# Three unsplit weight pieces of layer 0 become split ones, with their low parts made by ScalarE and an adding DMA

## The chip, the cores and the metric

The kernel runs on one core of a Trainium2 chip. The metric is the device time of one execution in microseconds; less is better. TensorE (PE in the profile) multiplies, VectorE (DVE) and ScalarE (ACT) do the elementwise work, GpSimd (POOL) and SyncE (SP) issue DMAs, and POOL adds up a few bias maps.

## The reference

Two layers of a decoder trunk on x of 256 tokens by 1024 features, in float32. Each layer:

```
mod = silu(c) @ w_mod[layer] + b_mod[layer];  shift, scale, gate = split(mod, 3)
hdn = rms_norm(x, norm_w[layer]) * (1 + scale) + shift
q1, k1, v1, g1, q2, k2, v2, g2 = split(hdn @ w_in[layer], 8)
y1, y2 = two attention branches (layer 0: differential and dilated; layer 1: block-sparse and stick-breaking)
y = concat([y1 * silu(g1), y2 * silu(g2)]) @ w_out[layer]
x = x + gate * y
```

The projections (ten column groups of 512 in each layer, K1, Q1, V1, K2, Q2, V2, G1, G2 and the two halves O0, O1 of the output) are most of TensorE's work.

## The kernel before

**Pieces and steps.** The weights are cut into 80 pieces, each 128 partitions by 1024 float32 (two blocks of 128 rows by 512 columns, 512 KB). A layer is 80 steps of TensorE. A step multiplies one piece with one half (side 0 or 1) of the activations, and most pieces are used in two steps. In layer 0, steps 24 to 31 are K2, 32 to 39 Q2, 40 to 47 V2, 48 to 55 G1, 56 to 63 G2 and 64 to 79 the output. Piece 12 + i belongs to steps 24 + 2i and 25 + 2i as far as piece 27; so piece 23 is used in steps 46 and 47 (V2, its last part), piece 25 in 50 and 51, piece 26 in 52 and 53 (both G1). Between the steps TensorE does the attention: scores of a pair of maps, transposes into the PSUM bank `turned`, products into the bank `mixed`.

**Split and plain pieces.** A split piece exists twice, as `w_hi` (rounded to fp32r) and `w_lo` (the rest); `mm3` (called in `project`) multiplies hi with hi, hi with lo and lo with hi, three fp32r matmuls. A piece in `PLAIN` is multiplied as it was loaded (`raw`) by one float32 matmul, which the profile shows as two. `split_hi(n)` (L478) lets ScalarE copy `raw` to `w_hi`, `split_lo(n)` (L751) lets VectorE subtract `w_hi` from `raw`. `w_hi` and `w_lo` have 8 slots each, which the pieces of `SPLIT` take in turn; `split_before(n)` is the one that held the slot. The copy is placed at the end of ScalarE's work for step `hi_at(n)`: 8 steps ahead of the first use, or as many as `EARLY` says, or in a step of `CHANGE_HI`. The subtraction stands in VectorE's work one step later (`lo_at`).

**What sets the order.** Every engine's program is unrolled step by step, each engine runs its own list in order, and semaphores connect them. ScalarE's list for step g begins with the copies out of `turned` (`take_turned`, L537 to L548) and `mixed` that TensorE filled in step g - 1, then come the exponentials of the attention maps (`exp_map`, L581), the squares of a finished group, and at its end the copies to `w_hi`. TensorE may not write `turned` again before ScalarE has emptied it (`turned_left`, L1090). The two transposes of K2 come after steps 36 and 37 (`TURN_QK`, L165), those of the normed heads (`turn_subln`) after steps 52 and 53 (`SUBLN_AT`).

**Loads.** SP issues one queue of loads into a ring of `RAW` = 7 buffers: pieces and 48 tiles of `w_mod`, which VectorE multiplies and sums in `take_mod` (L771), in the steps of `MOD_AT` (L180). The list is sorted (L404 and L405): a split piece by `hi_at`, a plain one by its first step, a `w_mod` tile by its step less one. Load i waits until the content of load i - 7 has been used: a `w_mod` tile by `take_mod`, a plain piece by the last of its steps, a split piece by `split_lo`. SP takes them strictly in this order. Four plain pieces (`HELD`) are instead loaded by POOL into `qT` and `kT` after step 59.

## Time and profile before

| | us |
|---|---|
| three runs, median | 324.62 |
| lowest and highest | 324.25, 324.77 |
| the profiled execution, its own time | 324.23 |
| its span, first to last instruction | 322.4 |

The profiled execution has 1.8 us outside its span and lies 0.4 us under the median. Busy are PE 299.4 us, DVE 235.2, ACT 196.9, POOL 16.2; TensorE's granted clock was 0.997 of full over the span. In a row of a timeline the first number is the start, the second the length from the first start to the last end of the merged instructions, and what stands in brackets is the idle time of the engine ahead of it and what ended that. A row of the chain of work gives start and length of a stretch on the path that ended last.

### The profile page before, as it was taken

How to read it: one execution, taken by the hardware profiler on the slowest of the kernel's cores; microseconds unless marked ns; L12 is line 12 of the kernel's file. 1: busy time of each engine (PE TensorE's matmuls, PEld its weight loads, DVE VectorE, ACT ScalarE, POOL GpSimd, SP SyncE). 2: the span in 40 equal slices, each digit the busy share in tenths (PEclk: the TensorE clock that was granted, in tenths of full speed). 3: DMA queues.
4: the chain of work that ended last, by engine and by line, in shares of the span. 5: the costliest groups of instructions: out<-in, count | busy, mean ns of one | idle time of the engine just before them, and what ended most of it. 6: DMA issues, size and time to landing. Idle time of an engine off the chain costs nothing.

```text
span 322.4 us, 4790 instructions
## 1 busy us (share of the span) xinstructions
PE 299.4 (93%) x1709; PEld 237.6 (74%) x1709; DVE 235.2 (73%) x480; ACT 196.9 (61%) x401; POOL 16.2 (5%) x24
## 2 busy tenths in 40 slices
PE   3498998999998999989999999999999999899995
PEld 2476876777555688886576888888987799798783
DVE  3898999998886697698957457989773547638633
ACT  3625568736745687998256446556664798959400
POOL 0000000000000942020000000000000000000000
PEclk9999999999999999999999999999999999999998
DMA  7999999495678958688752315679547148000011
GB/s 253 363 401 411 405 406 399 147 328 180 248 265 255 332 203 317 216 329 320 260 196 65 133 65 195 209 256 305 209 155 277 48 143 273 23 0 2 0 67 65
DMA packets 19879, 70.31 MB, mean 218 GB/s; under 512 B 2192, under 2 KB 2576, under 8 KB 19856
## 3 DMA queue, kind: packets, MB, share of 16 engines
q1 hardware_dynamic: 19280, 67.91, 58.4%
q0 software_dynamic: 576, 2.10, 1.7%
q8 instruction: 14, 0.23, 0.3%
q14 instruction: 9, 0.07, 0.1%
HBM read 68.95 MB, written 1.05 MB: 217 GB/s over the span
## 4 chain that ended last, share of the span: by engine, by line
PE 68%; DVE 12%; ACT 9%; DMA 5%; issue 3%; SPq 1%; ACTq 0%; DVEq 0%
PE proj L1082 46%; PE score L1082 13%; DMA raw<-in_w 5%; PE mixed L1082 5%; DVE raw L771 4%; DVE w_lo L751 3%; PE turned L1127 2%; ACT w_hi L478 2%; PE turned L1109 2%; DVE y L946 1%; DVE gt L938 1%; DVE probs L1021 1%; ACT y L502 1%; ACT gt L627 1%; SPq L449 1%
## 5 line engine op out<-in xcount | busy, mean ns | idle before, releaser
L751 DVE TENSOR_TENSOR w_lo<-raw,w_hi 128x1024 fp32r<-128x1024 f32 x68 | 82.3, 1222 | 14.1 <-ACT w_hi L478 13.6
L478 ACT ACTIVATE w_hi<-raw 128x1024 fp32r<-128x1024 f32 x68 | 70.6, 1050 | 17.8 <-DMA raw<-in_w 16.7
L1082 PE MATMUL proj<-w_hi,hy_hi 128*128 128x512 f32 x144 | 60.0, 417 | 4.8 <-DVE hy_lo L805 4.4
L771 DVE CUSTOM_DVE_ANT_0 raw<-raw,c_rows 128x1024 f32<-128x1024 f32 x48 | 59.0, 1251 | 0.0
L1082 PE MATMUL proj<-w_lo,hy_hi 128*128 128x512 f32 x144 | 56.9, 395 | 0.0
L1082 PE MATMUL proj<-w_hi,hy_lo 128*128 128x512 f32 x144 | 56.8, 394 | 0.0
L1082 PE MATMUL proj<-hy_hi,w_hi 128*128 128x256 f32 x176 | 52.5, 298 | 0.0
L1082 PE MATMUL proj<-hy_lo,w_hi 128*128 128x256 f32 x176 | 49.7, 283 | 0.0
L1082 PE MATMUL proj<-hy_hi,w_lo 128*128 128x256 f32 x176 | 49.7, 283 | 0.0
L1082 PEld LDWEIGHTS proj<-w_hi,hy_hi 128*128 128x128 f32 x144 | 27.5, 191 | 13.0 <-issue 3.9
L1082 PEld LDWEIGHTS proj<-hy_hi,w_hi 128*128 128x128 f32 x176 | 33.6, 191 | 2.1 <-issue 2.1
L1082 PEld LDWEIGHTS proj<-hy_lo,w_hi 128*128 128x128 f32 x176 | 33.6, 191 | 0.2 <-issue 0.2
L1082 PEld LDWEIGHTS proj<-hy_hi,w_lo 128*128 128x128 f32 x176 | 33.6, 191 | 0.0
L1082 PEld LDWEIGHTS proj<-w_hi,hy_lo 128*128 128x128 f32 x144 | 27.5, 191 | 6.1
L1082 PEld LDWEIGHTS proj<-w_lo,hy_hi 128*128 128x128 f32 x144 | 27.6, 191 | 5.4 <-issue 0.5
L581 ACT ACTIVATE probs<-logits,stat 128x128 f32<-128x128 f32 (+1 forms) x48 | 21.3, 446 | 6.7 <-DVE stat L853 6.7
L1082 PE MATMUL proj<-raw,y 128*128 128x512 f32 x48 | 22.4, 595 | 0.0
L548 ACT ACTIVATE probsT<-turned 128x384 f32<-128x384 f32 x20 | 9.7, 483 | 17.9 <-PE turned L1127 17.9
L890 DVE TENSOR_REDUCE n_ms<-sq 128x8 f32<-128x512 f32 (+1 forms) x13 | 9.4, 726 | 11.3 <-ACT sq L615 9.8
L1021 DVE SCALAR_TENSOR_TENSOR probs<-score,logits 128x384 f32<-128x384 f32 x8 | 4.1, 552 | 17.0 <-ACT logits L692 17.0
L1082 PE MATMUL score<-w_hi,hy_hi 128*128 128x512 f32 x40 | 16.1, 402 | 0.0
L1082 PE MATMUL score<-w_lo,hy_hi 128*128 128x512 f32 x40 | 15.6, 390 | 0.0
(147 smaller groups left out, 439.8 us busy)
## 6 DMA issues: line engine op xcount, KB each, us to landing
raw<-in_w SPq DMA_DIRECT2D x76, 512.0 KB, 4.7
raw<-in_w_mod SPq DMA_DIRECT2D x48, 512.0 KB, 5.7
xs<-in_x SPq DMA_DIRECT2D x1, 1024.0 KB, 5.2
qT<-in_w POOLq DMA_DIRECT2D x2, 512.0 KB, 6.5
kT<-in_w POOLq DMA_DIRECT2D x2, 512.0 KB, 8.4
out_x<-xs SPq DMA_DIRECT2D x4, 256.0 KB, 2.0
cst<-in_constants SPq DMA_DIRECT2D x1, 520.0 KB, 6.3
logits<-in_a_lambda SPq DMA_DIRECT2D x1, 128.0 KB, 12.1
```

The costliest lines, as they stand in the source:

```text
L449: sp.dma_start(raw_tile(key), whence.rearrange("p (k n) -> p k n", k=2)).then_inc(raw_full[i % RAW], 16)
L478: nc.scalar.activation(w_hi[:, slot(n), :, :], raw_tile(("w", n)), ACT.Copy).then_inc(hi_done, 1)
L502: j = nc.scalar.activation(y[:, k, :], b[:, i * S:(i + 1) * S], ACT.Identity, scale=v[:, V_A + k:V_A + k + 1], bias=v[:, V_B + k:V_B + k + 1])
L548: nc.scalar.activation(probsT[:, (2 * j + o) % 4, :], turned[:, 0:MAPW], ACT.Copy).then_inc(turn_act, 1)
L581: i = nc.scalar.activation(probs[:, M % 4, cs], logits[:, M % 2, cs], ACT.Exp, scale=-1.0, bias=st[:, tile:tile + 1], accum_out=st[:, 2 + ...
L751: nc.vector.tensor_tensor(w_lo[:, slot(n), :, :], raw_tile(("w", n)), w_hi[:, slot(n), :, :], ALU.subtract).then_inc(lo_done, 1)
L771: nc.vector.tensor_tensor_reduce(out=tile, in0=tile, in1=c_rows[:, :], scale=1.0, scalar=0.0, op0=ALU.mult, op1=ALU.add, accum_out=col(V_M ...
L890: nc.vector.reduce_sum(n_ms[:, n % 2, heads * s:heads * s + heads], src.rearrange("p (h d) -> p h d", h=heads), axis=AX.X).then_inc(ms_ok, 1)
L1021: nc.vector.scalar_tensor_tensor(out=probs[:, (2 * i + o) % 4, :], in0=score[o][:, 0:MAPW], scalar=0.0, in1=logits[:, o, :], op0=ALU.max, ...
L1082: return nc.tensor.matmul(o, a, b, start=start, stop=stop, skip_group_check=True)
L1109: i = nc.tensor.transpose(turned[:, b * P:(b + 1) * P], qn[:, s, b * P:(b + 1) * P], ident)
L1127: i = nc.tensor.transpose(turned[:, b * P:(b + 1) * P], probs[:, (2 * j + o) % 4, b * P:(b + 1) * P], ident)
```

## The change

- Pieces 23, 25 and 26 leave `PLAIN` and become split pieces; a new list `SUMMED` names them. Their copies to `w_hi` are placed by `SUMMED_HI` in the steps 33, 36 and 37.
- Their low part is not made by VectorE. Right behind the copy, ScalarE waits for it and writes `w_lo` = -`w_hi` (a second copy with scale -1). POOL waits for that (`neg_ok`) and issues a DMA that reads the piece once more from HBM and adds it into `w_lo` (`accum_op` add). Three such DMAs stand at the start of POOL's list. TensorE waits for the landing (`summed_in`) instead of for VectorE.
- SP may refill the ring buffer of such a piece once its `w_hi` copy is done.
- In `EARLY`, three entries change: the high part of piece 27 moves from step 38 to 41, that of 28 from 43 to 45, that of 29 from 45 to 47 (with three more split pieces each slot comes free later). Their subtractions on VectorE move along, from 39, 44 and 46 to 42, 46 and 48.
- The keys by which loads are sorted change with it: 23, 25 and 26 are loaded at places 40, 45 and 47 of the queue (before 57, 61 and 64), and the entries between move back. The plain piece 19, used from step 38 on, goes from place 45 to 48, so from behind the release of load 38 (the `w_mod` tile of step 30) to behind that of load 41, which now is the `w_mod` tile of step 35. Piece 20 goes from 48 to 50, 21 from 51 to 54, 22 from 54 to 56.

```diff
--- before.py
+++ after.py
@@ -68,7 +68,10 @@
 
 HELD = (34, 37, 38, 39)
 HELD_FROM = 59
-PLAIN = (18, 19, 20, 21, 22, 23, 25, 26, 34, 37, 38, 39)
+PLAIN = (18, 19, 20, 21, 22, 34, 37, 38, 39)
+
+SUMMED = (23, 25, 26)
+SUMMED_HI = (33, 36, 37)
 SPLIT = [n for n in range(len(FIRST)) if n not in PLAIN]
 
 
@@ -86,6 +89,11 @@
     return SPLIT.index(n) + 1
 
 
+def lo_count(n):
+
+    return sum(m not in SUMMED for m in SPLIT[:SPLIT.index(n) + 1])
+
+
 def done_at(layer, c, side):
 
     return STEPS * layer + max(g for g, (cc, p, s) in enumerate(STEP[layer]) if (cc, s) == (c, side))
@@ -109,7 +117,7 @@
 
 
 
-EARLY = {24: 14, 27: 16, 28: 13, 29: 12, 30: 10, 31: 9, 32: 12, 33: 11, 35: 12, 36: 10,
+EARLY = {24: 14, 27: 13, 28: 11, 29: 10, 30: 10, 31: 9, 32: 12, 33: 11, 35: 12, 36: 10,
          72: 12, 73: 12, 74: 12, 75: 11, 78: 4, 79: 4}
 
 CHANGE_HI = {40: 67, 41: 68, 42: 69, 43: 70, 44: 74, 45: 76, 46: 79, 47: 80}
@@ -119,6 +127,8 @@
 def hi_at(n):
     if n < 12:
         return FIRST[n] - 6
+    if n in SUMMED:
+        return SUMMED_HI[SUMMED.index(n)]
     return CHANGE_HI.get(n, max(FIRST[n] - EARLY.get(n, 8), LAST[split_before(n)] + 1))
 
 
@@ -132,7 +142,7 @@
 
 
 def pieces_lo(layer, g):
-    return [n for n in SPLIT if lo_at(n) == STEPS * layer + g]
+    return [n for n in SPLIT if n not in SUMMED and lo_at(n) == STEPS * layer + g]
 
 
 
@@ -394,6 +404,8 @@
         y_ok, y_hi_ok, y_lo_ok = sem("y_ok"), sem("y_hi_ok"), sem("y_lo_ok")
         upd, out_ok, stored = sem("upd"), sem("out_ok"), sem("stored")
         dve_step = sem("dve_step")
+        neg_ok = sem("neg_ok")
+        summed_in = [sem(f"summed_in{i}") for i in range(len(SUMMED))]
         held_in = [sem(f"held_in{i}") for i in range(len(HELD))]
 
 
@@ -443,8 +455,10 @@
                         n = was[1]
                         if n in PLAIN:
                             wait_step(sp, LAST[n])
+                        elif n in SUMMED:
+                            sp.wait_ge(hi_done, split_count(n))
                         else:
-                            sp.wait_ge(lo_done, split_count(n))
+                            sp.wait_ge(lo_done, lo_count(n))
                 whence = w_mod[mods.index(key[1])] if key[0] == "mod" else w[key[1]]
                 sp.dma_start(raw_tile(key), whence.rearrange("p (k n) -> p k n", k=2)).then_inc(raw_full[i % RAW], 16)
                 if key == ("w", 2):
@@ -476,6 +490,10 @@
                 if split_before(n) is not None:
                     wait_step(act, LAST[split_before(n)])
                 nc.scalar.activation(w_hi[:, slot(n), :, :], raw_tile(("w", n)), ACT.Copy).then_inc(hi_done, 1)
+                if n in SUMMED:
+                    act.wait_ge(hi_done, split_count(n))
+                    nc.scalar.activation(w_lo[:, slot(n), :, :], w_hi[:, slot(n), :, :], ACT.Copy,
+                                         scale=-1.0).then_inc(neg_ok, 1)
 
             def h_hi(n, blocks, ts):
 
@@ -1061,6 +1079,10 @@
 
         @block.gpsimd
         def _(pool):
+            for i, n in enumerate(SUMMED):
+                pool.wait_ge(neg_ok, i + 1)
+                nc.gpsimd.dma_start(w_lo[:, slot(n), :, :], w[n].rearrange("p (k n) -> p k n", k=2),
+                                    accum_op=ALU.add).then_inc(summed_in[i], 16)
             pool.wait_ge(cst_in, 16)
             wait_turned(pool, ("qk", 0, Q2, 1))
             for M in range(8, 16):
@@ -1269,8 +1291,10 @@
                 if at == FIRST[n]:
                     if plain:
                         wait_raw(pe, ("w", n))
+                    elif n in SUMMED:
+                        pe.wait_ge(summed_in[SUMMED.index(n)], 16)
                     else:
-                        pe.wait_ge(lo_done, split_count(n))
+                        pe.wait_ge(lo_done, lo_count(n))
                 if p == 0:
                     was = before_in_bank(layer, c, s)
                     if was:
```

ScalarE from behind the seed of K2's norm (end of step 33) to the end of step 38, before. `L537 kT<-turned` are the two copies that empty `turned` after K2's two transposes:

```order
L561 ACTIVATE gt<-mixed,stat 128x128 x2
L478 ACTIVATE w_hi<-raw 128x1024
L548 ACTIVATE probsT<-turned 128x384
L581 ACTIVATE probs,stat<-logits,stat 128x128
L581 ACTIVATE probs,stat<-logits,stat 128x256
L537 ACTIVATE kT<-turned,v 128x4x128
L581 ACTIVATE probs,stat<-logits,stat 128x128
L581 ACTIVATE probs,stat<-logits,stat 128x256
L537 ACTIVATE kT<-turned,v 128x4x128
L561 ACTIVATE gt<-mixed,stat 128x128 x2
L478 ACTIVATE w_hi<-raw 128x1024
```

The same stretch now, where L492 is `w_hi`, L495 the new `w_lo<-w_hi`, L555 the copy to `kT`:

```order
L492 ACTIVATE w_hi<-raw 128x1024
L495 ACTIVATE w_lo<-w_hi 128x1024
L579 ACTIVATE gt<-mixed,stat 128x128 x2
L492 ACTIVATE w_hi<-raw 128x1024
L566 ACTIVATE probsT<-turned 128x384
L599 ACTIVATE probs,stat<-logits,stat 128x128
L599 ACTIVATE probs,stat<-logits,stat 128x256
L492 ACTIVATE w_hi<-raw 128x1024
L495 ACTIVATE w_lo<-w_hi 128x1024
L555 ACTIVATE kT<-turned,v 128x4x128
L599 ACTIVATE probs,stat<-logits,stat 128x128
L599 ACTIVATE probs,stat<-logits,stat 128x256
```

and on, without a gap:

```order
L492 ACTIVATE w_hi<-raw 128x1024
L495 ACTIVATE w_lo<-w_hi 128x1024
L555 ACTIVATE kT<-turned,v 128x4x128
L579 ACTIVATE gt<-mixed,stat 128x128 x2
L633 ACTIVATE sq<-proj2 128x512
```

Six instructions have come in: a pair ahead of `gt<-mixed`, a pair ahead of the first `kT<-turned`, a pair ahead of the second. The `w_hi` copy of piece 27, which stood behind the second `gt<-mixed`, has gone.

ScalarE in steps 47 to 50, before. `L607 val<-proj1` ends the V2 group, `L471` ends the seed for the normed heads:

```order
L607 ACTIVATE val<-proj1 128x512
L581 ACTIVATE probs,stat<-logits,stat 128x128
L581 ACTIVATE probs,stat<-logits,stat 128x256
L467 ACTIVATE n_y<-n_ms,v 128x8
L469 ACTIVATE n_y<-n_y 128x8
L471 ACTIVATE n_t<-n_y 128x8
L478 ACTIVATE w_hi<-raw 128x1024
L590 ACTIVATE probs<-probs,stat 128x128
L590 ACTIVATE probs<-probs,stat 128x256
L590 ACTIVATE probs<-probs,stat 128x128
```

and now:

```order
L492 ACTIVATE w_hi<-raw 128x1024
L625 ACTIVATE val<-proj1 128x512
L599 ACTIVATE probs,stat<-logits,stat 128x128
L599 ACTIVATE probs,stat<-logits,stat 128x256
L481 ACTIVATE n_y<-n_ms,v 128x8
L483 ACTIVATE n_y<-n_y 128x8
L485 ACTIVATE n_t<-n_y 128x8
L492 ACTIVATE w_hi<-raw 128x1024
L608 ACTIVATE probs<-probs,stat 128x128
L608 ACTIVATE probs<-probs,stat 128x256
L608 ACTIVATE probs<-probs,stat 128x128
```

The `w_hi` copy of piece 29 has come in between the square of `gt` and `val<-proj1`.

## Rows read from the trace of the kernel before

**Rows 1.** The page's first section: busy us, share, instructions of each engine.
```profile
PE 299.4 (93%) x1709; PEld 237.6 (74%) x1709; DVE 235.2 (73%) x480; ACT 196.9 (61%) x401; POOL 16.2 (5%) x24
```
**Rows 2.** Chain that ended last, steps 37 to 39: start us, us, what.
```profile
82.88 1.72 PE proj L1082 x4
84.60 0.44 PE turned L1109 x4
85.03 0.67 PE mixed L1082 x6
85.70 3.44 PE proj L1082 x8
```
**Rows 3.** Timeline of ACT, 76 to 86 us: start us, us, engine, line, what, [idle before].
```profile
76.65 0.62 ACT L561 ACTIVATE gt<-mixed,stat 128x128 f32<-128x128 f32 x2
77.17 1.06 ACT L478 ACTIVATE w_hi<-raw 128x1024 fp32r<-128x1024 f32 x1
80.76 0.49 ACT L548 ACTIVATE probsT<-turned 128x384 f32<-128x384 f32 x1 [2.53 <-PE turned L1127]
82.58 0.40 ACT L581 ACTIVATE probs<-logits,stat 128x128 f32<-128x128 f32 x1 [1.33 <-DVE stat L853]
...
83.48 0.67 ACT L537 ACTIVATE kT<-turned,v 128x512 f32<-128x512 f32 x1
...
85.07 0.69 ACT L537 ACTIVATE kT<-turned,v 128x512 f32<-128x512 f32 x1
```
**Rows 4.** Timeline of DVE, 79 to 82 us.
```profile
79.63 1.22 DVE L751 TENSOR_TENSOR w_lo<-raw,w_hi 128x1024 fp32r<-128x1024 f32 x1
80.77 1.22 DVE L771 CUSTOM_DVE_ANT_0 raw<-raw,c_rows 128x1024 f32<-128x1024 f32 x1
```
**Rows 5.** Timeline of all engines, 99.3 to 100.4 us.
```profile
99.38 0.69 ACT L537 ACTIVATE qT<-turned,v 128x512 f32<-128x512 f32 x1 [0.61 <-PE turned L1109]
...
100.21 0.41 PE L1127 MATMUL turned<-cst,probs 128*128 128x128 f32 x2 [0.87 <-ACT qT L537]
```
**Rows 6.** Timeline of SP's issues, and, for `raw` at 60 to 100 us, issue to landing.
```profile
72.04 5.29 SPq L449 DMA_DIRECT2D raw<-in_w  x2
82.02 0.33 SPq L449 DMA_DIRECT2D raw<-in_w_mod  x1
```
```profile
DMA to landing us min/median/max: 3.3/4.5/6.7
```
**Rows 7.** Chain that ended last: a split step by tokens, a plain and a split by columns.
```profile
60.73 1.39 PE proj L1082 x6
...
120.81 1.73 PE proj L1082 x8
...
218.53 1.44 PE proj L1082 x12
```
**Rows 8.** Timeline of ACT, 110 to 122 us (steps 47 to 53).
```profile
111.29 0.58 ACT L607 ACTIVATE val<-proj 128x512 f32<-128x512 f32 x1
...
113.36 1.04 ACT L478 ACTIVATE w_hi<-raw 128x1024 fp32r<-128x1024 f32 x1
114.30 1.48 ACT L590 ACTIVATE probs<-probs,stat 128x128 f32<-128x128 f32 x4
...
117.98 0.40 ACT L581 ACTIVATE probs<-logits,stat 128x128 f32<-128x128 f32 x1 [0.87 <-DVE stat L853]
...
121.07 0.67 ACT L542 ACTIVATE y<-turned,v 128x512 f32<-128x512 f32 x1
```
**Rows 9.** Timeline of DVE, 113 us.
```profile
113.48 0.17 DVE L756 SCALAR_TENSOR_TENSOR n_t<-n_ms,n_t 128x8 f32<-128x8 f32 x1 [0.54 <-ACT n_t L471]
```
**Rows 10.** Chain that ended last: the two transposes of the normed heads.
```profile
120.37 0.44 PE turned L1119 x4
...
122.54 0.44 PE turned L1119 x4
```
**Rows 11.** DMA issues by line: engine op xcount, KB each, median us to landing.
```profile
qT<-in_w POOLq DMA_DIRECT2D x2, 512.0 KB, 6.5
kT<-in_w POOLq DMA_DIRECT2D x2, 512.0 KB, 8.4
```

## The prediction

> **What bounds the kernel now.** I read the page's shares first: TensorE is busy 93% of the span, the next engine 73% [rows 1], and the clock was 0.997. A change pays if it shortens TensorE's work where TensorE is the last to be ready, and it costs wherever it lets TensorE wait. So next I read the chain of work around the places that the change touches. From step 37 on it is one unbroken TensorE stretch: projection, transpose of K2, product, projection, each starting where the one before ends [rows 2]. Every microsecond that TensorE waits there is a microsecond of the kernel, since ScalarE and VectorE take their later work from TensorE. Then I read what ScalarE does in the same time, to see how much room it has [rows 3]: it is idle for 2.53 us before 80.76 and for 1.33 us before 82.58, in the second case because VectorE's logits are not there. Then comes the row that matters most: `kT<-turned` starts at 83.48, and TensorE's next transpose, which needs that bank empty, at 84.60. The room is below one microsecond.
>
> **The gain: shorter steps.** The pieces 23, 25 and 26 feed steps 46, 47 and 50 to 53. A plain step takes 1.72 us by tokens [rows 2] and 1.73 by columns, a split one 1.39 and 1.44 [rows 7]. That is 2 x 0.33 + 4 x 0.29 = 1.82 us less TensorE work. VectorE gets none of it, since the low parts are made elsewhere.
>
> **The cost in steps 33 to 38: two copies per piece on ScalarE.** A copy to `w_hi` takes 1.06 us [rows 3]. The negation has the same shape and I give it the same time: the first of the pair must end before it starts (1.06, and 0.03 for the wait), the second lets its successor start 0.1 before its end, so a pair costs 1.06 + 0.03 + 0.95 = 2.04 us. The replay, in times of the trace:
> - Pair 23 (step 33) goes ahead of `gt<-mixed`, which started at 76.65, and the copy of piece 24, which started at 77.17 [rows 3]. That copy now runs 79.19 to 80.25. The idle 2.53 us behind it take this in for ScalarE and for `probsT` at 80.76, but VectorE subtracts piece 24 from 79.63 on [rows 4] and now must wait to 80.27: 0.64 us late. VectorE has no gap ahead of the next logits, so ScalarE's exponentials start at 83.2 instead of 82.58.
> - Pair 25 (step 36) stands behind these exponentials and ahead of the first `kT<-turned`. 82.58 + 0.64 + 0.90 (the exponentials: 83.48 - 82.58) = 84.12; pair to 86.16; so the copy starts at 86.16 instead of 83.48.
> - TensorE starts 0.83 us after the start of such a copy (99.38 to 100.21, where it did wait for one) [rows 5]. So the second K2 transpose starts at 86.99; in the chain TensorE was ready at 84.60, and its first row in the timeline is some 0.15 before that. Against 84.43 the loss is 2.56 us. Without VectorE's delay (if it caught up) it would be 1.92: that is the lower end.
> - Pair 26 (step 37) delays the second `kT<-turned` to about 89.7, but TensorE needs `turned` again only after steps 38 and 39, at 89.14 + 2.56 = 91.7. This one is hidden, by the 3.44 us of projections [rows 2]. With the cover gone it would cost up to its 2.04.
>
> Nothing absorbs the 2.56 later: ScalarE and VectorE wait for TensorE's transposes and scores after 90 us, and none of them gets them earlier. The moved copy of 27 (38 to 41) lies in ScalarE's idle time and costs nothing; 28 takes the place of 29 in step 45.
>
> **The cost in steps 47 to 53: piece 29 moved.** Its `w_hi` copy now stands in step 47, in front of `val<-proj1`, which started at 111.29 [rows 8]. Back to back it costs 0.95. ScalarE had no gap from there to 116.6: `val`, exponentials, the seed, the copy of 30, `probs`, the copy of 31. Its one gap, 0.87 us before 117.98, is a wait for VectorE's logits, and VectorE in turn had waited for ScalarE's seed at 113.48 [rows 9] and then worked without a gap. So the gap moves along and hides nothing. ScalarE starts this run 0.33 us earlier, since step 46 is 0.33 shorter; the net is 0.62 late. Its copy of the normed heads out of `turned` starts at 121.07 + 0.62 = 121.69 [rows 8], TensorE's second transpose of them at 121.69 + 0.83 = 122.52. Before, it started at 122.54 [rows 10]. TensorE would by then have been 0.66 + 4 x 0.29 = 1.82 us ahead, and stands where it stood: the whole gain of the short steps is spent waiting for ScalarE. What is late next is ScalarE, no longer TensorE's arithmetic. I take 0.0 for this stretch. Bounds: if ScalarE were not in the way, -1.82; if the second gap were lost too, +0.3.
>
> **The adding DMAs.** The trace has no such DMA. The nearest rows are POOL's plain loads of the same 512 KB, 6.5 and 8.4 us to landing [rows 11]. The negations end near 78.8, 86.2 and 89.7, the users start at 106, 113 and 118 plus the shift: over 25 us of room each, three times those rows. I take 0. The other end: each us beyond the room costs one.
>
> **The queue of loads.** Piece 19 was issued at 72.04; now it goes behind the release of the `w_mod` tile that VectorE takes at 80.77 [rows 4, 6], which frees the buffer at 82.02 (the issue that waited for it before), 82.66 with VectorE's 0.64. With 3.3 to 6.7 us to landing [rows 6] it is there at 86.0 to 89.4. Step 38 began at 85.70 and begins, after the loss at K2, at 88.26. So at the median, 4.5 (87.2), it is just hidden by the wait for ScalarE; at the upper end it adds 1.1 us. The two do not add up, the larger counts. Without ScalarE's delay it would cost 0.3 to 3.7 us alone, so taking that wait away would not give it all back. Pieces 20 to 22 have a few us more.
> In the Trainium skill, DMA: Bandwidth & Descriptors, under Issuing engines are not separate DMA queues, DMAs of all issuing engines run on the same 16 DMA engines and interleave. By that the first adding DMA, in flight from about 79 on, would lengthen this very load, and the sum would go to its upper end, +1.1; no row here shows the two side by side.
>
> **Sum.** 324.23 (profiled execution: span 322.4 and 1.8 around it) + 2.56 + 0.0 = 326.8. The median of the runs lies 0.4 above the profiled one, so I forecast 327.1 us, slower by 0.8%.
>
> **Rivals.**
> 1. Piece 19 is the last to be ready, not ScalarE: 327.1 + 1.1 = 328.2, up to 329.5 if the adding DMA holds it up longer than any load in [rows 6]. For it: a load moved from 12 us ahead to a few. Against: the median just fits.
> 2. Part of the gain survives: if VectorE gives back its 0.64 and half of the 1.82 is kept in steps 46 to 53, 327.1 - 0.64 - 0.9 = 325.6. For it: the stretch of [rows 8] is tied together by gaps of tenths of a us.
> 3. Faster: the gain comes through and ScalarE is not late at K2. That is the case if the first `kT<-turned` starts before 84.60 - 0.83 = 83.8. It needs pair 25 to run inside the 1.33 us gap before 82.58, but the list has the pair behind the exponentials, and piece 19 would still cost its 0.3 us. Price: 324.6 - 1.82 + 0.3 = 323.1. The mechanism decides at one point and the order speaks against it.
> 4. The adding DMAs land later than 25 us: TensorE waits at step 46, 330 or more.
>
> **How the numbers follow.** Forecast 0.58 (326.2 to 327.8), rival 1 0.16, rival 2 0.12, rival 3 0.10, rival 4 0.04. The likeliest gives 327.1. The range takes in the forecast, rival 1 and most of rival 2: 325.3 to 329.0. A measurement of this kernel tells about 0.2% (0.65 us) from no change: rival 2 gives 0.07 of its 0.12 to no change and 0.05 to slower; the faster side is rival 3. So faster 0.11, same 0.08, slower 0.81.
>
> **What would show it.** In the changed kernel's profile TensorE should be idle for some 2.5 us ahead of the second transpose of K2 (near 87 us), released by ScalarE's `kT` copy, and ScalarE's rows ahead of it should be exponentials, `w_hi`, `w_lo`, `kT`. If the release is a DMA ahead of a float32 projection instead, rival 1 holds. Steps 46, 47 and 50 to 53 should be 0.3 us shorter, with TensorE's new waits at `turned` between steps 50 and 53 adding up to about as much. The forecast is wrong if the negation takes much less than 1.06 us, if `kT` starts near 84, or if no new wait appears between 115 and 125 us.

## The result, and the profile after

| | before | changed |
|---|---|---|
| runs | 4 | 4 |
| median, us | 324.67 | 333.80 |
| lowest and highest, us | 324.25, 324.77 | 331.56, 335.56 |
| the profiled execution, its own time, us | 324.23 | 335.56 |
| its span, us | 322.4 | 333.8 |

The changed kernel is slower by 2.8%: the ratio of the times is 1.0282, with a 95% interval of 1.0251 to 1.0313. The direction was forecast; the size was not. 333.8 us lies well above the range of 325.3 to 329.0. A second set of runs of the same kernel (`r_after`, below) gave 333.59 against 324.52 us.

The profiled execution is the longest of its four. The spans of the two profiles differ by 11.4 us, the medians by 9.1. I come back to that difference below.

The page's first section of the changed kernel, which answers to [rows 1]; TensorE is busy 2.7 us longer, although its arithmetic got less, because part of it ran at the lower clock, as shown below:

```profile
PE 302.1 (91%) x1729; PEld 239.4 (72%) x1729; DVE 235.5 (71%) x480; ACT 202.5 (61%) x407; POOL 19.7 (6%) x27
```

The granted clock of that span is 0.983, where it was 0.997. Line numbers have moved: L1104 is the projection that was L1082, L1131 the transposes of K2 and Q2, L1149 those of the probabilities, L1141 those of the normed heads, L555 the copy out of `turned`. Here is TensorE's timeline of the stretch from step 36 to step 42 (start us, us, engine, line, what, and in brackets the idle time ahead of it and what ended that). It answers to [rows 2], where no row waits:

```profile
84.64 0.60 PE L1131 MATMUL turned<-cst,qn 128*128 128x128 f32 x4
85.08 1.88 PE L1104 MATMUL proj<-raw,y 128*128 128x512 f32 x4
89.22 0.63 PE L1131 MATMUL turned<-cst,qn 128*128 128x128 f32 x4 [2.26 <-ACT kT L555]
89.69 0.83 PE L1104 MATMUL mixed<-val,probsT 128*128 128x128 f32 x6
90.36 5.29 PE L1104 MATMUL proj<-raw,y 128*128 128x512 f32 x8
...
96.82 3.60 PE L1104 MATMUL proj<-raw,y 128*128 128x512 f32 x8
100.26 0.83 PE L1104 MATMUL mixed<-val,probsT 128*128 128x128 f32 x6
103.85 3.53 PE L1104 MATMUL proj<-raw,y 128*128 128x512 f32 x4 [2.76 <-DMA raw<-in_w]
107.17 1.24 PE L1104 MATMUL mixed<-cst,v 128*128 128x128 f32 x8
108.25 1.88 PE L1104 MATMUL proj<-raw,y 128*128 128x512 f32 x4
```

Four things are in these rows. The wait for ScalarE's `kT` is the forecast one. Behind it eight projections take 5.29 us, where the same eight take 3.60 a few us later. Then TensorE waits 2.76 us for a load, that of piece 21 (step 42). Behind that wait four projections take 3.53 us, where four take 1.88. The two long rows are the engine's lower clock. These are windows of 4 us (window; busy us of PE, PEld, DVE, ACT, POOL; granted clock; DMA share; GB/s):

```profile
88.00:92.00 4.00, 2.78 (x13) 1.78 (x14) 1.95 (x5) 3.97 (x9) 0.88 (x1) 0.81 0.94 345
92.00:96.00 4.00, 4.00 (x13) 1.73 (x13) 1.02 (x3) 1.68 (x4) 0.86 (x1) 0.76 0.97 234
96.00:100.00 4.00, 4.00 (x17) 1.99 (x14) 2.30 (x11) 2.95 (x12) 0.00 (x0) 1.00 1.07 275
...
104.00:108.00 4.00, 4.00 (x10) 1.98 (x11) 4.00 (x8) 0.00 (x0) 0.00 (x0) 0.57 0.74 262
```

A mean of 0.5 would be the lower level, 1.2 GHz, throughout; 0.57 is nearly that.

The chain of work that ended last says the same with its own words (start us, us, what):

```profile
86.47 0.96 ACT w_hi L492
...
87.45 0.05 ACT w_lo L495
...
88.41 0.67 ACT kT L555
...
92.73 11.07 DMA raw<-in_w
103.80 0.04 issue
103.85 3.53 PE proj L1104 x4
```

The load of piece 21 took 11.1 us from issue to landing; no `raw` load issued between 60 and 100 us took more than 6.7 before [rows 6]. What the DMA engines did meanwhile is in the DMA view of 80 to 107 us (queue: packets, MB, share of 16 engines). Before, and then changed:

```profile
DMA packets 1935, 7.10 MB, mean 263 GB/s; under 512 B 206, under 2 KB 206, under 8 KB 1933
q1 hardware_dynamic: 1933, 7.07, 75.2%
```
```profile
DMA packets 2173, 7.94 MB, mean 294 GB/s; under 512 B 239, under 2 KB 239, under 8 KB 2171
q1 hardware_dynamic: 1739, 6.34, 63.6%
q0 software_dynamic: 432, 1.57, 31.5%
```

Queue q0 is POOL's: the three adding DMAs, 1.57 MB in 432 packets. The time of their packets is 31.5% of what the 16 engines have in 27 us, or 8.5 us of all 16. SP's 6.34 MB take 63.6%, 17.2 us. So a MB costs 5.4 us by adding and 2.7 us by plain loads, and the engines are now 95% busy where they were 75%. By line, the adding DMAs land after this many us at the median, against 6.5 and 8.4 of the plain ones [rows 11]:

```profile
w_lo<-in_w POOLq DMA_DIRECT2D x3, 512.0 KB, 9.3
```

**Where the 11.4 us of the two profiles lie.** For each step I took the time at which TensorE's last matmul of the step signals, subtracted that of the profile of before, and noted by how much this delay grows between two marks (positive is slower). The waits for `kT` at the second K2 transpose fall into column 38, those for piece 21 into 42–45:

| kernel | to 37 | 38 | 39–41 | 42–45 | 46–47 | 48–50 | 51–54 | rest | sum |
|---|---|---|---|---|---|---|---|---|---|
| changed | 2.37 | 4.06 | 0.09 | 4.72 | -0.65 | -0.29 | 1.11 | 0.01 | 11.4 |
| `r_after` | 1.13 | 2.45 | 0.00 | 7.34 | -0.65 | -0.28 | 1.11 | -0.01 | 11.1 |
| `e_plain_dma` | 0.86 | 4.11 | 0.00 | 0.27 | -0.65 | -0.28 | 1.12 | -0.02 | 5.4 |
| `e_no_neg` | 0.03 | 1.62 | 1.78 | 6.45 | -0.65 | -0.29 | 1.11 | -0.01 | 10.0 |
| `e_dve_low` | 1.06 | 1.96 | 0.00 | 1.71 | -0.65 | -0.28 | 1.11 | 0.01 | 4.9 |
| `e_29_back` | 0.10 | 2.47 | 0.00 | 6.17 | -0.65 | -0.29 | 0.28 | 0.01 | 8.1 |
| `e_late_add` | 1.05 | 2.46 | 0.00 | 0.97 | -0.65 | -0.28 | 3.61 | -0.03 | 7.1 |
| `v_add` | 0.81 | 0.00 | 4.10 | 0.00 | -0.64 | -0.28 | 0.28 | 0.03 | 4.3 |
| `v_plain_placed` | 0.54 | 0.00 | 1.91 | 0.00 | -0.66 | -0.28 | 1.63 | 0.08 | 3.2 |
| `v_add_late` | 0.13 | 0.00 | 0.00 | 1.60 | -0.66 | -0.28 | 3.48 | 0.01 | 4.3 |
| `v_dve_placed` | 0.28 | 0.00 | 0.00 | 0.25 | -0.65 | -0.28 | 4.74 | 0.07 | 4.4 |
| `v_g1_add` | -0.02 | 0.00 | 0.00 | 0.00 | 4.67 | -0.29 | -0.53 | 0.00 | 3.8 |
| `v_g1_dve` | 0.70 | 0.00 | 0.00 | 0.00 | 1.43 | -0.30 | -0.16 | 0.01 | 1.7 |
| `v_two` | 0.46 | 0.00 | 0.00 | -0.65 | -0.66 | 0.01 | 1.34 | 0.00 | 0.5 |
| `e_early_only` | 0.89 | 0.00 | 0.00 | 0.00 | 0.00 | 0.00 | 0.45 | 0.03 | 1.4 |

The first column is not the change. It arises before step 24, while the first loads arrive, and scatters from -0.02 to 2.37 us over kernels that are alike there; the two profiles of the same changed kernel differ by 1.24 in it. The other columns of the changed kernel sum to 9.04 us, close to the 9.1 of the medians; those of `r_after` sum to 9.97, where its medians differ by 9.07. Both profiles are of the longest of their four executions, so a single profile fixes these sums to about 1 us only. Behind step 54 nothing happens: the delay is only carried along.

### The profile page after: what moved, and what is told of

Same layout as the page of the kernel before. It is cut to its first block, busy times and chain, and to the rows that moved or that the text cites. A ratio compares the mean times of both kernels' runs of the same rounds, so it can differ in the third digit from the quotient of the medians.

```text
span 333.8 us, 4842 instructions
## 1 busy us (share of the span) xinstructions
PE 302.1 (91%) x1729; PEld 239.4 (72%) x1729; DVE 235.5 (71%) x480; ACT 202.5 (61%) x407; POOL 19.7 (6%) x27
## 3 DMA queue, kind: packets, MB, share of 16 engines
HBM read 70.52 MB, written 1.05 MB: 214 GB/s over the span
## 4 chain that ended last, share of the span: by engine, by line
PE 55%; ACT 14%; DMA 13%; DVE 11%; issue 4%; SPq 1%; ACTq 0%; DVEq 0%
PE proj L1104 36%; DMA raw<-in_w 13%; PE score L1104 12%; PE mixed L1104 4%; ACT w_hi L492 3%; DVE w_lo L769 3%; DVE raw L789 2%; ACT probs L599 2%; PE turned L1149 2%; PE turned L1131 1%; DVE y L964 1%; DVE gt L956 1%; DVE logits L871 1%; SPq L463 1%; DVE probs L1039 1%
## 5 line engine op out<-in xcount | busy, mean ns | idle before, releaser
L492 ACT ACTIVATE w_hi<-raw 128x1024 fp32r<-128x1024 f32 x71 | 73.7, 1049 | 19.2 <-DMA raw<-in_w 18.0
L1104 PE MATMUL proj<-w_hi,hy_hi 128*128 128x512 f32 x148 | 61.6, 416 | 5.6 <-DVE hy_lo L823 5.2
L1104 PE MATMUL proj<-w_lo,hy_hi 128*128 128x512 f32 x148 | 58.5, 395 | 0.0
L1104 PE MATMUL proj<-w_hi,hy_lo 128*128 128x512 f32 x148 | 58.5, 395 | 0.0
L1104 PE MATMUL proj<-hy_hi,w_hi 128*128 128x256 f32 x192 | 56.8, 296 | 0.0
L1104 PE MATMUL proj<-hy_lo,w_hi 128*128 128x256 f32 x192 | 54.2, 282 | 0.0
L1104 PE MATMUL proj<-hy_hi,w_lo 128*128 128x256 f32 x192 | 54.2, 282 | 0.0
L1104 PEld LDWEIGHTS proj<-w_hi,hy_hi 128*128 128x128 f32 x148 | 28.2, 190 | 14.3 <-issue 4.5
L1104 PEld LDWEIGHTS proj<-hy_hi,w_hi 128*128 128x128 f32 x192 | 36.6, 191 | 1.9 <-issue 1.9
L1104 PEld LDWEIGHTS proj<-hy_lo,w_hi 128*128 128x128 f32 x192 | 36.7, 191 | 0.0
L1104 PEld LDWEIGHTS proj<-hy_hi,w_lo 128*128 128x128 f32 x192 | 36.6, 191 | 0.0
L1104 PEld LDWEIGHTS proj<-w_hi,hy_lo 128*128 128x128 f32 x148 | 28.2, 190 | 6.3
L1104 PEld LDWEIGHTS proj<-w_lo,hy_hi 128*128 128x128 f32 x148 | 28.2, 191 | 5.5 <-issue 0.5
L1104 PE MATMUL proj<-raw,y 128*128 128x512 f32 x40 | 21.8, 684 | 2.8 <-DMA raw<-in_w 2.8
L908 DVE TENSOR_REDUCE n_ms<-sq 128x8 f32<-128x512 f32 (+1 forms) x13 | 9.3, 725 | 12.7 <-ACT sq L633 11.3
L1104 PE MATMUL score<-w_hi,hy_hi 128*128 128x512 f32 x40 | 16.1, 402 | 0.0
L1104 PE MATMUL score<-w_hi,hy_lo 128*128 128x512 f32 x40 | 15.6, 390 | 0.0
```

The source lines that it names most:

```text
L492: nc.scalar.activation(w_hi[:, slot(n), :, :], raw_tile(("w", n)), ACT.Copy).then_inc(hi_done, 1)
L908: nc.vector.reduce_sum(n_ms[:, n % 2, heads * s:heads * s + heads], src.rearrange("p (h d) -> p h d", h=heads), axis=AX.X).then_inc(ms_ok, 1)
L1104: return nc.tensor.matmul(o, a, b, start=start, stop=stop, skip_group_check=True)
```

## The experiments

Ratios are to the kernel before, run on the same chip in the same set. Its medians were 324.52, 324.49, 324.6 and 324.45 us in the four sets.

**The same kernel again.** No edit.

> The changed kernel again, as the base for the others. Its first profile was 11.4 us longer in span than before: 2.4 us up to step 25, 2.4 us of waiting for ScalarE's kT copy at K2, 1.7 us in steps 38 and 39 at the lower TensorE clock, 2.9 us of waiting for piece 21, 1.8 us at the lower clock behind it, and 0.2 more to the end. If the first 2.4 us are the change's doing, they return here; if they are scatter of the loads at the start, this profile has less of it, and the time lies near 331.5. The other terms should return within some tenths of a us in both cases.

Measured: 333.59 us (332.4 to 335.24), ratio 1.0265 (1.0234 to 1.0296). Its TensorE rows at the two waits:

```profile
87.98 0.63 PE L1131 MATMUL turned<-cst,qn 128*128 128x128 f32 x4 [2.25 <-ACT kT L555]
...
89.11 3.60 PE L1104 MATMUL proj<-raw,y 128*128 128x512 f32 x8
...
103.18 3.78 PE L1104 MATMUL proj<-raw,y 128*128 128x512 f32 x4 [5.03 <-DMA raw<-in_w]
```

The wait for `kT` is the same to 0.01 us. The 2.4 us ahead of step 24 did not all return (1.13), so they are scatter; but the time did not fall to the expected 331.5, because the wait for piece 21 was longer. Here the clock stays up behind the wait for `kT` (3.60). TensorE then comes to piece 21 earlier and waits longer. The split between the clock and the wait for the load differs between these two profiles; that piece 21 is late does not (nor in `e_29_back`, where the wait for it is 4.24 us).

**Is it the adding?** In the first kernel the three DMAs only copy, so `w_lo` holds the whole piece instead of its low part:

```diff
-                nc.gpsimd.dma_start(w_lo[:, slot(n), :, :], w[n].rearrange("p (k n) -> p k n", k=2),
-                                    accum_op=ALU.add).then_inc(summed_in[i], 16)
+                nc.gpsimd.dma_start(w_lo[:, slot(n), :, :], w[n].rearrange("p (k n) -> p k n", k=2)).then_inc(summed_in[i], 16)
```

> The three DMAs of POOL are plain copies and do not add, so the low parts of pieces 23, 25 and 26 are wrong; sizes and waits are as in the changed kernel. Theory A (the adding packets, 328 ns each against 159 for a plain one of the same 4096 bytes, fill the DMA engines and make piece 21 late): the copies take 3 x 8 x 0.17 = 4 us less of every engine, piece 21 lands in time or 1 us late, the wait of 2.8 us and the lower clock behind it go: 3 to 4.5 us faster than the changed kernel. Theory B (piece 21 is late because it stands further back in SP's queue and its buffer is released late): the wait stays, less than 1 us faster.

Measured: 329.38 us, ratio 1.0136 (1.0104 to 1.0168), 4.2 us less than `r_after`. TensorE waits for no load any more. The queues from 79 to 106 us:

```profile
q1 hardware_dynamic: 1765, 6.44, 66.2%
q0 software_dynamic: 432, 1.57, 16.3%
```

The same 432 packets now hold the engines for 16.3% of 27 us, 4.4 us instead of 8.5. The difference of 4.1 us is near the 4.2 that the kernel gained, but the two are not the same thing: engine time is not TensorE's waiting, and in the table column 42–45 falls by 7.1 against `r_after` while the lower clock behind `kT` puts 1.66 into column 38. The order of the loads is that of the changed kernel, and piece 21 was issued as early on the same scale (91.22 less 0.86, against 91.48 less 1.13 in `r_after`); it landed after 8.3 us instead of 11.7. So the adding decides here whether TensorE waits, not the later place alone. The plain copies are not free either: the loads issued from 87.2 to 94.1 took 6.4 to 8.3 us. What is left of 1.0136 in the profile is mostly the wait for `kT` with the lower clock behind it (4.11 in the table).

In the second kernel the second and third adding DMA are issued later, when TensorE has passed step 41:

```diff
                 pool.wait_ge(neg_ok, i + 1)
+                if i == 1:
+                    wait_step(pool, 41)
```

> The changed kernel, where POOL's second and third adding DMA wait for the end of step 41. ScalarE, the queue of loads and the amount of work are unchanged. Theory A (the adding packets make piece 21 late, which is needed right behind step 41): the wait of 2.8 to 5 us for piece 21 and the lower clock behind it go, 4 to 6 us faster than the changed kernel, unless the adding DMAs now collide with piece 22 (step 44), which would give 1 to 3 us of it back. Theory B (the place in the queue): no gain.

Measured: 330.56 us, ratio 1.0178 (1.0152 to 1.0204), 3 us less than `r_after` (2.8 by the ratios). The wait for piece 21 fell to 0.71 us; it landed after 7.3 us instead of 11.7, so these two DMAs held that load up by some 4 us. They now hold up the next ones. ScalarE's `w_hi` copy of piece 28, and TensorE 11 us later behind the chain of copy, logits and probabilities:

```profile
111.65 1.06 ACT L492 ACTIVATE w_hi<-raw 128x1024 fp32r<-128x1024 f32 x1 [2.67 <-DMA raw<-in_w]
```
```profile
122.75 0.55 PE L1151 MATMUL turned<-cst,probs 128*128 128x128 f32 x3 [3.09 <-ACT probs L608]
```

Moving the DMAs moves the collision.

**Is it ScalarE's second copy?** First without the negation; POOL issues the adding DMA right behind the `w_hi` copy, onto whatever the slot held:

```diff
-                if n in SUMMED:
-                    act.wait_ge(hi_done, split_count(n))
-                    nc.scalar.activation(w_lo[:, slot(n), :, :], w_hi[:, slot(n), :, :], ACT.Copy,
-                                         scale=-1.0).then_inc(neg_ok, 1)
...
-                pool.wait_ge(neg_ok, i + 1)
+                pool.wait_ge(hi_done, split_count(n))
```

> ScalarE does not write -w_hi; POOL adds the piece to whatever the slot held, right behind the w_hi copy, so the low parts are wrong. Each pair on ScalarE shrinks from 2.04 to 1.05 us. By the replay of ScalarE's list the first kT copy starts near 84.4 of the old time instead of 86.2, so the wait at K2 falls from 2.4 to about 0.8 us, and if the lower clock of steps 38 and 39 comes from that wait, 1.7 us more go: 3 to 3.5 us faster than the changed kernel. If the clock falls at such short waits too, only 1.6 us faster. If piece 19 is the next to be late, 1 us faster. The wait for piece 21 should stay.

Measured: 333.79 us, ratio 1.027 (1.023 to 1.0309): no gain at all. TensorE's rows with a wait:

```profile
85.25 0.63 PE L1126 MATMUL turned<-cst,qn 128*128 128x128 f32 x4 [0.63 <-ACT kT L550]
...
87.08 3.70 PE L1099 MATMUL proj<-raw,y 128*128 128x512 f32 x8 [0.53 <-DMA raw<-in_w]
...
93.63 3.70 PE L1099 MATMUL proj<-raw,y 128*128 128x512 f32 x8 [1.52 <-DMA raw<-in_w]
...
101.53 3.78 PE L1099 MATMUL proj<-raw,y 128*128 128x512 f32 x4 [3.54 <-DMA raw<-in_w]
```

The wait for `kT` fell from 2.26 to 0.63 us, as it should, and waits for pieces 19, 20 and 21 took its place; these loads took 5.0, 8.7 and 12.7 us. Taking ScalarE's delay away gained nothing, since the loads set the time. The experiment is not clean, though. Without the negation the adding DMAs also start sooner and closer together: the second and third were issued 2.37 us apart (84.85 and 87.22) instead of 3.46, and the loads issued from 84.9 to 90.8 took 8.7 to 13.2 us. So part of what ScalarE gave back may have been lost to a denser collision. What the negation costs by itself is not shown.

Then the other way round: the same steps, but no negation and no DMA. VectorE subtracts, as for every other split piece (all lines on `neg_ok` and `summed_in` go).

```diff
-    return [n for n in SPLIT if n not in SUMMED and lo_at(n) == STEPS * layer + g]
+    return [n for n in SPLIT if lo_at(n) == STEPS * layer + g]
```

> Pieces 23, 25 and 26 split in the usual way: w_hi on ScalarE in the same steps, w_lo by VectorE one step later, no negation and no adding DMA. If the adding DMAs and the negations are the cause, this is 5 us or more faster than the changed kernel, about 327. VectorE has 3 x 1.22 us more in steps 34 to 38, where it is 86 percent busy, so its logits and the release of the buffer for piece 19 come 1 to 2.4 us later: a rival says that this wait is as long as what it replaces, and the time stays above 330.

Measured: 329.66 us, ratio 1.0164 (1.0124 to 1.0204).

```profile
87.43 0.63 PE L1119 MATMUL turned<-cst,qn 128*128 128x128 f32 x4 [1.77 <-ACT kT L547]
99.04 1.99 PE L1092 MATMUL proj<-raw,y 128*128 128x512 f32 x4 [1.44 <-DMA raw<-in_w]
```

The usual way of splitting is 4 us cheaper than the adding one at these places, and still 1.6% slower than before. This lies between the recorded 327 and the rival's 330. The wait for `kT` is now VectorE's doing: the exponentials ahead of it start at 84.78, behind a wait of 2.47 us for VectorE's logits, which stand behind two subtractions instead of one. Piece 21 is late even with no POOL DMA in flight. It landed after 5.9 us, which is within the 3.3 to 6.7 of [rows 6], but it was issued only at 93.11. Less the 1.06 of the first column that is 1.7 us later than in the changed kernel (92.73 less 2.37). SP's row ahead of it, at place 53, had waited for VectorE to be done with a `w_mod` tile (92.7 us), and VectorE does that behind one of its new subtractions. So this wait is not the one of the changed kernel, and it does not show that the place in the queue was the cause there.

**The three entries of `EARLY`.** Alone in the kernel before, and taken back in the changed kernel:

```diff
-EARLY = {24: 14, 27: 16, 28: 13, 29: 12, 30: 10, 31: 9, 32: 12, 33: 11, 35: 12, 36: 10,
+EARLY = {24: 14, 27: 13, 28: 11, 29: 10, 30: 10, 31: 9, 32: 12, 33: 11, 35: 12, 36: 10,
```

> The kernel before with nothing but the three changed entries of EARLY: the high parts of pieces 27, 28 and 29 go to steps 41, 45 and 47. The prediction's replay says that the copy of 29 in step 47 costs ScalarE 0.95 us, of which up to 0.3 us remain at TensorE by step 54 where nothing else is shorter: 324.6 to 325.2. If the copy lies in idle time after all, no change; if every wait behind it lengthens, 325.6.

> The changed kernel with the three entries of EARLY as they were (27 in step 38, 28 in 43, 29 in 45). From step 45 to 54 the changed kernel gained 1 us and gave it back, +0.18 us in all against before. Without the copy of 29 in step 47 ScalarE empties the normed heads 0.95 us earlier, so this stretch should end at -0.6 to -0.8. The waits ahead of step 45 (ScalarE at K2, piece 21) stay, with piece 27 ahead of 20 and 21 in the queue: the time 0.8 us lower than the changed kernel's, or more than that higher if piece 21 comes later still.

Measured: 324.99 us, ratio 1.0011 (0.9998 to 1.0024), with 0.45 us between steps 50 and 54; and 332.85 us, ratio 1.0257 (1.0229 to 1.0285), with 0.28 instead of 1.11 us there. By the medians neither is clear of noise; by the profiles the three moved copies cost 0.8 us when TensorE's steps are short and 0.45 when they are not, against 0.95 and at most 0.3 in the replay. That it is the copy of piece 29 in step 47 is the replay's reading; the three were not moved one by one. `e_29_back` also shows that the three pieces don't force these moves: the text on the change said that each slot comes free later, but the kernel runs as well with the old entries. What the changed kernel does need is that the `w_hi` copies come in the order of their pieces, since they are counted.

**Other places.** Four kernels keep the three split pieces but move the copies out of the way of `kT`, with `EARLY` as before. `HI_ORDER` counts the copies in the order in which they are made. `v_add`:

```diff
-SUMMED_HI = (33, 36, 37)
+SUMMED_HI = (35, 39, 42)
...
-    return SPLIT.index(n) + 1
+    return HI_ORDER.index(n) + 1
...
+HI_ORDER = sorted(SPLIT, key=hi_at)
```

> The same three pieces, negations and adding DMAs, but the pairs on ScalarE in steps 35, 39 and 42, where the trace of before has it idle for 2.5, 2.5 and 2.0 us, pieces 27, 28 and 29 in their old steps 38, 43 and 45, and the loads sorted accordingly (piece 19 one place behind its old one). If placement was the fault of the change, the wait at K2 (2.3 us) and the lateness of piece 19 go: 326 or less. The adding DMAs now start near 80, 90 and 97 us, so the third can still make piece 21 or 22 late; if the adding packets are a cause of their own, 1 to 4 us of wait for a load remain and the time is 326 to 329.

Measured: 327.75 us, ratio 1.0099 (1.0083 to 1.0115). No wait for `kT`, but

```profile
93.42 5.40 PE L1107 MATMUL proj<-raw,y 128*128 128x512 f32 x8 [2.14 <-DMA raw<-in_w]
```

a wait for piece 20 with the lower clock behind it: 2.14 + 1.80 (5.40 - 3.60) of the 4.10 us of steps 39 to 41. `v_plain_placed` is the same with plain copies for the adding DMAs:

> v_add with POOL's three DMAs as plain copies, so the low parts of pieces 23, 25 and 26 are wrong; the places, the negations and the waits are those of v_add (pairs in steps 35, 39, 42). v_add was 3.2 us slower than before, by a wait for piece 20 and the lower clock behind it. If the length of the adding packets is the cause, piece 20 is in time and 0.6 us of the gain of the short steps show: 324.0 to 324.6. If it is any extra load from POOL at this place (the same bytes at the plain rate), a wait of 1 us or more for piece 20, 21 or 22 stays and the time is 325.5 to 327.5.

Measured: 327.55 us, ratio 1.0095 (1.0065 to 1.0126): no better.

```profile
92.65 3.70 PE L1106 MATMUL proj<-raw,y 128*128 128x512 f32 x8 [1.64 <-DMA raw<-in_w]
...
118.73 0.55 PE L1151 MATMUL turned<-cst,probs 128*128 128x128 f32 x3 [1.12 <-ACT probs L611]
```

Here the adding is not what costs: the difference of 0.2 us is within noise. Whether it is the extra bytes or the new order of the loads these two don't tell. `v_add_late` makes all three copies late, adding, and `v_dve_placed` does the same with VectorE's subtraction and no DMA of POOL's (`SUMMED_HI = (39, 42, 44)` in both):

> All three pieces with negation and adding DMA, pairs on ScalarE in steps 39, 42 and 44 instead of 35, 39 and 42. v_add lost 2.1 us to piece 20 and as much again to the lower clock behind it. Here the first adding DMA starts near 93, so it cannot meet piece 20; it may meet 21 or 22. If the collision just moves along with the adding DMAs, the time is again 327 to 329; if the loads have room there, 324.0.

> All three pieces split in the usual way, w_hi in steps 39, 42 and 44, w_lo by VectorE one step later, no negation and no DMA from POOL. Nothing is read twice. If the adding DMAs and ScalarE's pair at K2 were all that was wrong, 0.5 us faster than before, 324.0. If the re-sorted queue alone makes a load late (piece 22 now waits for the buffers of others), a wait of about 1 us for it, 324.8 to 326.

Measured: 328.66 us, ratio 1.0116 (1.0099 to 1.0133), and 327.36 us, ratio 1.0084 (1.0054 to 1.0113); the second is above both of its recorded cases. In `v_dve_placed` ScalarE waits for two loads and TensorE in the end for ScalarE:

```profile
103.99 1.06 ACT L491 ACTIVATE w_hi<-raw 128x1024 fp32r<-128x1024 f32 x1 [1.21 <-DMA raw<-in_w]
...
109.72 1.06 ACT L491 ACTIVATE w_hi<-raw 128x1024 fp32r<-128x1024 f32 x1 [4.09 <-DMA raw<-in_w]
```
```profile
119.73 0.55 PE L1140 MATMUL turned<-cst,probs 128*128 128x128 f32 x3 [4.03 <-ACT probs L603]
```

These are pieces 26 and 29. This kernel loads no byte more than the one before. The split pieces must be in their buffers some steps ahead of their use, so they are loaded earlier and others later. That, with three more copies on ScalarE and three more subtractions on VectorE, costs 0.8% here; no run parts the three.

**Fewer pieces.** `v_two` splits 22 and 23 (copies in steps 42 and 44), `v_g1_dve` 25 and 26 (the same steps), both by VectorE; `v_g1_add` is the latter by negation and adding DMA. Their edit to the kernel before, `v_two` and `v_g1_dve` in turn, beside `HI_ORDER`:

```diff
+PLAIN = (18, 19, 20, 21, 25, 26, 34, 37, 38, 39)
+SUMMED = (22, 23)
...
+PLAIN = (18, 19, 20, 21, 22, 23, 34, 37, 38, 39)
+SUMMED = (25, 26)
+SUMMED_HI = (42, 44)
```

> The kernel before with two pieces of V2, 22 and 23, split in the usual way (w_hi in steps 42 and 44 on ScalarE, w_lo one step later on VectorE), pieces 25 and 26 plain, EARLY as before. Steps 44 to 47 get 0.33 us shorter each, 1.3 us in all; VectorE has 3.6 us of idle time ahead of step 46 to take 2.4 us more. If ScalarE and VectorE are the bound behind step 46 as the replay says, 0.3 to 1 us of it is kept: 323.6 to 324.3. If their new work delays the logits of step 46, no change. Slower if piece 21 or 22 comes late.

> The kernel before with pieces 25 and 26 alone split in the usual way: w_hi on ScalarE in steps 42 and 44, where it is idle for 2.0 and 1.6 us, w_lo on VectorE one step later, ahead of its 3.6 us of idle time. EARLY as before, piece 23 plain. Steps 50 to 53 get 0.29 us shorter each, 1.16 in all. ScalarE's list behind step 46 is as before, and the stretch up to step 54 is bound by its copies: in v_add 0.64 us of the gain was left there. So 0.6 us faster than before, 323.9. No change if VectorE's logits come late, slower if a load does.

> The same two pieces with negation and adding DMA (the change's way), pairs on ScalarE in steps 42 and 44. VectorE has nothing more to do. If the adding packets are a cause of their own, they meet the loads of piece 23 (plain, needed at step 46, landed 0.4 us ahead of it before) or of piece 29: a wait of 1 to 5 us for a load, 325 to 328. If two adding DMAs at this place find room, 0.6 us faster than before, as v_g1_dve.

Measured, each but the last over 12 runs: `v_two` 324.47 us, ratio 0.9998 (0.9988 to 1.0009); `v_g1_dve` 325.28, ratio 1.002 (1.0005 to 1.0034); `v_g1_add` 328.0, ratio 1.0105 (1.0087 to 1.0123). `v_two` is 1.31 us ahead by step 47 and gives back 1.35 by step 54, at the copies of the probabilities and of the normed heads. `v_g1_dve` keeps 0.46 us in steps 48 to 54 and loses 1.43 in steps 46 and 47, where it waits 1.16 us for piece 23. With the adding DMA the same wait is 2.82 us, and the lower clock behind it brings the loss to 4.67 us. The two kernels load in the same order and move no other copy, so their ratios (1.002 and 1.0105) compare the two ways of making the low part most directly, with the negation and the adding together:

```profile
108.96 2.48 PE L1107 MATMUL proj<-raw,y 128*128 128x512 f32 x4 [2.82 <-DMA raw<-in_w]
```

None of these kernels beats the one before. `v_two` and `v_g1_dve` were expected to be 0.3 to 1 us and 0.6 us faster.

## Why the prediction was wrong in size

**The gain: shorter steps.** Right. Steps 46 and 47 are shorter by 0.64 to 0.66 together in every kernel with piece 23 split (forecast 0.66), and a split step still takes 1.39 us, as in [rows 7].

**The cost in steps 33 to 38.** Right in its size and nearly in its working. Forecast was a wait for ScalarE of 2.56 us at the second K2 transpose; it is 2.26 in the row, and 2.45 to 2.47 in step 38 of the three profiles with full clock behind it. ScalarE's rows, which answer to [rows 3]:

```profile
78.90 1.04 ACT L492 ACTIVATE w_hi<-raw 128x1024 fp32r<-128x1024 f32 x1
79.97 1.06 ACT L495 ACTIVATE w_lo<-w_hi 128x1024 fp32r<-128x1024 f32 x1
80.94 0.61 ACT L579 ACTIVATE gt<-mixed,stat 128x128 f32<-128x128 f32 x2
...
85.48 0.40 ACT L599 ACTIVATE probs<-logits,stat 128x128 f32<-128x128 f32 x1 [1.87 <-DVE stat L871]
...
86.38 1.04 ACT L492 ACTIVATE w_hi<-raw 128x1024 fp32r<-128x1024 f32 x1
87.45 1.06 ACT L495 ACTIVATE w_lo<-w_hi 128x1024 fp32r<-128x1024 f32 x1
88.41 0.67 ACT L555 ACTIVATE kT<-turned,v 128x512 f32<-128x512 f32 x1
```

The negation takes the assumed 1.06 us, the pair costs 2.04 (80.94 - 78.90), the exponentials 0.90, and TensorE starts 0.81 us behind `kT`. VectorE's logits delay ScalarE by 0.53 us instead of 0.64 (85.48 - 82.58, less the 2.37 by which everything was late already); that is about the 0.1 by which the loss is smaller. What the step left out is that such a wait can be followed by the lower clock. It cost 1.69 us (5.29 - 3.60) in this profile and 1.66 in that of `e_plain_dma` (4.11 - 2.45), and nothing in `r_after`, `e_29_back` and `e_late_add`, with the same wait to 0.03 us. I had read the clock of before, 0.997, and then never asked what would become of it.

**The cost in steps 47 to 53.** Right: from step 46 to 54 the changed kernel's delay grows by 0.17 us (-0.65 - 0.29 + 1.11) where I took 0.0 with bounds of -1.82 and +0.3. The whole gain is spent waiting for ScalarE, at the places that [rows 10] named:

```profile
126.95 0.55 PE L1149 MATMUL turned<-cst,probs 128*128 128x128 f32 x3 [0.55 <-ACT probs L608]
...
131.35 0.63 PE L1141 MATMUL turned<-cst,gt 128*128 128x128 f32 x4 [0.34 <-ACT probsT L566]
...
133.75 0.63 PE L1141 MATMUL turned<-cst,gt 128*128 128x128 f32 x4 [0.34 <-ACT y L560]
```

`e_early_only` and `e_29_back` agree with that: 0.45 us alone, 0.8 us with the short steps.

**The adding DMAs.** This is the step that failed: the term "I take 0". I held the DMAs against their own users only, with 25 us of room. That part is true: no TensorE wait in any kernel was for `summed_in`. But a DMA also costs those who share the engines with it, and the price is per byte twice that of a load: 8.5 us of all 16 engines for 1.57 MB, against 4.4 as plain copies. Making them plain gave the kernel 4.2 us back. The nearest rows [rows 11] gave the time to landing, which says nothing about that. A hint that I could have used stands in the Trainium skill, Collectives: The Full Stack, under The bandwidth ceiling: the fold count and why AG ≠ RS ≠ AR: in a ring ReduceScatter between cores the adding step reads two operands, so it puts twice the reads of AllGather's copy on the same ring per byte delivered. That is about collectives and not about a DMA into SBUF, but the trace agrees with the factor: 31.5% to 16.3% of 27 us is 1.93.

**The queue of loads.** Half right. Piece 19 was issued at 84.92 and landed at 88.18, ahead of TensorE. Less the 2.37 us of the first column that is 82.55 and 85.8, where I had 82.66 and 86.0 to 89.4. Wrong was to price only this one load, and the sentence "Pieces 20 to 22 have a few us more". Piece 20 did. Piece 21 had been issued at 87.43 before, for a projection that began at 94.41: 7 us of room, of which it used 4.4. Now it was issued at 92.73 for a projection that could have begun at 101.09: 8.4 us of room, so more than before, and it took 11.1 us. Its room had not shrunk; its landing had grown. The loads issued from 88.7 to 95.7 all took 8.5 to 11.1 us, while two adding DMAs, issued at 88.82 and 92.28, were in flight (with plain copies the same loads took 6.4 to 8.3):

```profile
88.82 0.88 POOL L1084 DMA_DIRECT2D w_lo<-in_w  x1 [6.45 <-ACT w_lo L495]
92.28 0.86 POOL L1084 DMA_DIRECT2D w_lo<-in_w  x1 [2.59 <-ACT w_lo L495]
```

The wait costs 2.76 us plus 1.65 of lower clock (3.53 - 1.88) here, 5.03 plus about 1.9 in `r_after`. For the sharing of the 16 engines I had cited the Trainium skill, DMA: Bandwidth & Descriptors, and concluded that piece 19 would be lengthened. That did not happen: it landed 3.27 us after its issue, the shortest of [rows 6], although the first adding DMA landed only at 86.80 (it took 4.04 us in `r_after`, 5.0 in `e_no_neg`). The rule struck at loads that I had not looked at, behind the second and third DMA.

**The rivals.** Rival 1 (a load is the last to be ready) is nearest, but at piece 21 and behind the wait for ScalarE instead of in its place: the two waits come one after the other, in different steps. Rivals 2 and 3 did not happen, and rival 4 did not either, though its "330 or more" is where the time came out: the DMAs it names landed in time, and their neighbours did not.

**Slips in the working.** 324.23 + 2.56 + 0.4 is 327.2 and not 327.1; 77.17 + 2.04 is 79.21 and not 79.19; piece 19 was issued 13.7 us ahead of step 38 and landed 9 us ahead, not 12; and the shares of the cases put 0.83 on slower, not 0.81. None of them bears on the miss.

**What each cause is worth.** Taking the adding away gives 4.2 us of 9.1. The other 4.9 are, in the profile of that kernel, the wait for `kT` and the clock behind it (4.11), with no wait for a load. The causes are not a sum: without the negation alone the time did not fall (but see above), without adding and negation it fell by 3.9, no more than without adding, because VectorE's work made new waits, and with the copies out of the way of `kT` (`v_add`) 3.3 us were left. What is left open: why adding packets hold the engines about twice as long (two reads would explain the factor, but no profile here counts the second one), and why the same 2.26 us wait lowers the clock in some executions and not in others.

## What to carry to other kernels

Before adding a DMA, look at the share of the DMA engines in the window in which it runs, not at the time its user can wait: here 75% was busy, and what was added took 32%. Then follow each load behind it to its first use, with the room that it has left after the queue's re-sorting. And do not count a new wait of TensorE at its length alone: in this kernel the lower clock behind one of 2.3 us added 1.7 us or nothing. Last, when a kernel without one of two causes is no faster, look at whether the edit moved the other: here it made the adding DMAs start sooner.

## What the runs showed of the hardware

- A DMA that adds 512 KB of float32 from HBM into an fp32r tile holds the 16 engines for about 2.8 us (8.5 / 3), a plain copy of the same size by the same queue for 1.5 (4.4 / 3). The adding ones landed after 9.3 and 11.0 us at the median in the two profiles of the changed kernel, the plain ones beside the same loads after 7.7.
- SP's loads issued while two such DMAs were in flight landed after 8.5 to 11.1 us, in `r_after` after 9.0 to 11.7 and in `e_no_neg` after up to 13.2, where 3.3 to 6.7 was usual [rows 6]. Beside plain copies they took 6.4 to 8.3 us, and with no DMA of POOL's (`e_dve_low`) 4.9 to 6.7.
- ScalarE's copy with a scale of -1 from an fp32r tile costs the same 1.06 us as the rounding copy from float32.
- TensorE's granted clock fell towards 1.2 GHz in or behind waits of 2.14 to 5.03 us in nine of the profiles; in the projection rows shown of the changed kernel, `r_after`, `e_no_neg` and `v_add` that cost 1.65 to 1.90 us, in that of `v_g1_add` 0.60, with the rest in later rows. It stayed up behind waits of 2.25 to 2.28 us in three profiles and behind one of 3.09 us (`e_late_add`).
